# Moving the last unit's value convolution and gated product from the up stage into the down stage of a decoder layer

## The reference, cut to what matters

```
h = rmsnorm(x, norm_ffn_pre)
up = causal_depthwise_conv(h @ w_up, conv_w, conv_b)   # 3 taps: y[t] = b + w0*h[t-2] + w1*h[t-1] + w2*h[t]
gate, val = up[..., :D_FF], up[..., D_FF:]             # D_FF = 2816
f = (silu(gate) * val) @ w_down
x = x + rmsnorm(f, norm_ffn_post)
```

## Time and profile before

| | |
|---|---|
| runs | 2508.09, 2510.10, 2510.82 us; median 2510.1 us |
| the profiled execution's own time | 2507.04 us |
| its span (first to last instruction) | 2505.4 us |
| mean granted clock of TensorE | 0.978 |
| PE busy, share of the span | 94% |
| DVE, ACT, POOL busy | 73%, 49%, 40% |

### The profile page before, as it was taken

The page is one execution under the profiler, slowest core; times in us unless marked ns, Lnnn a source line. Parts: engine busy times, 40 slices in busy tenths (PEclk is TensorE's granted clock), DMA queues, the critical chain, the costliest instruction groups (busy, mean ns, idle before and its releaser), DMA issues. The chain is left out here.

```text
span 2505.4 us, 37528 instructions
## 1 busy us (share of the span) xinstructions
PE 2350.7 (94%) x11661; PEld 1950.1 (78%) x11661; DVE 1830.5 (73%) x2141; ACT 1226.5 (49%) x2101; POOL 1005.9 (40%) x747
## 2 busy tenths in 40 slices
PE   6989999989999979996999999899999989999987
PEld 5767887878888877884888888678888868888865
DVE  4424222989999976887998998999999963344687
ACT  4412112879898974555444444544444433333444
POOL 0000001786666642556454554455454520121463
PEclk9999999999999999997999999999999999999999
DMA  7932337143333315778233332633233334445566
GB/s 232 289 89 75 127 117 198 55 127 85 87 95 89 90 35 159 236 217 260 85 105 100 109 105 84 206 101 105 84 113 105 96 114 151 160 175 174 173 208 240
DMA packets 297728, 341.53 MB, mean 136 GB/s; under 512 B 13508, under 2 KB 219004, under 8 KB 292476
## 3 DMA queue, kind: packets, MB, share of 16 engines
q1 hardware_dynamic: 295292, 331.50, 42.9%
q0 software_dynamic: 2304, 8.39, 0.8%
HBM read 213.48 MB, written 109.58 MB: 129 GB/s over the span
## 5 line engine op out<-in xcount | busy, mean ns | idle before, releaser
L764 POOL TENSOR_TENSOR weight<-beta,stick 128x512 f32<-128x512 f32 (+3 forms) x320 | 304.2, 958 | 572.0 <-ACT beta L717 450.8
L1968 DVE SCALAR_TENSOR_TENSOR x<-up_cols,taps,x 128x1024 f32<-128x1024 f32 x176 | 259.2, 1473 | 16.2 <-ACT x L1870 13.0
L811 DVE TENSOR_TENSOR_SCAN stick<-z_ps,stick,beta 128x512 f32<-128x512 f32 x192 | 245.5, 1279 | 10.9 <-ACT z_ps L718 9.7
L540 PE MATMUL out_ps<-hT,w_hi 128*128 128x512 f32 x768 | 239.7, 393 | 9.8 <-DVE w_lo L474 9.8
L1955 DVE TENSOR_TENSOR wu_lo<-wu_sums,wu_hi 128x512 fp32r<-128x512 f32 x175 | 216.4, 1237 | 0.0
L717 ACT ACTIVATE beta<-z_ps 128x512 f32<-128x512 f32 (+3 forms) x320 | 171.2, 535 | 59.2 <-PE z_ps L841 52.5
L1857 ACT ACTIVATE wu_hi<-wu_sums 128x512 fp32r<-128x512 f32 x175 | 109.6, 628 | 170.0 <-PE gate_odd_ps L2079 91.1
L2079 PE MATMUL value_chain_ps<-wide,wu_hi 128*128 128x512 f32 x528 | 178.5, 392 | 9.9 <-DVE up_cols L2026 9.6
L540 PEld LDWEIGHTS out_ps<-hT,w_hi 128*128 128x128 f32 x768 | 145.2, 189 | 42.0 <-DVE w_lo L474 10.3
L858 PE MATMUL wT_ps<-ident,weight 128*128 128x128 f32 x1088 | 173.3, 275 | 3.1 <-POOL weight L764 3.1
L718 ACT ACTIVATE z_ps<-z_ps 128x512 f32<-128x512 f32 (+3 forms) x320 | 172.0, 538 | 0.0
(11 more groups left out here) (239 smaller groups left out, 6201.5 us busy)
## 6 DMA issues: line engine op xcount, KB each, us to landing
wu_f<-in_w_up SPq DMA_DIRECT2D x44, 512.0 KB, 4.9
bridge<-in_w_up SPq DMA_DIRECT2D x44, 512.0 KB, 4.9
f_scratch<-f_sum SPq DMA_DIRECT2D x88, 256.0 KB, 2.0
down_lo<-f_scratch SPq DMA_DIRECT2D x44, 512.0 KB, 3.3
down_b<-in_w_down SPq DMA_DIRECT2D x76, 256.0 KB, 3.7
f_scratch<-x SPq DMA_DIRECT2D x66, 256.0 KB, 2.1
x_scratch<-x SPq DMA_DIRECT2D x56, 256.0 KB, 2.8
first_head<-qk_scratch SPq DMA_DIRECT2D x24, 512.0 KB, 9.7
```

The lines of the kernel that those rows point to most:

```text
L540: m = pe.matmul(out_ps[half + j][:, :], w[slot][:, k, :], hT[h][:, k, j * BANK:(j + 1) * BANK], start=(k == 0 and t == 0), stop=(k == kc - ...
L764: pool.tensor_tensor(weight[v % weight_ring][:, 0:w], beta[v % stick_in][:, 0:w], stick[q % 2][:, at:at + w], ALU.mult).then_inc(weight_do ...
L811: dve.tensor_tensor_scan(stick[q % 2][:, at:at + w][:, ::-1], backwards, beta[u % stick_in][:, 0:w], start, ALU.mult, ALU.bypass).then_inc ...
L1968: dve.scalar_tensor_tensor(out=conv[h], in0=cols[:, h, 2 - back:2 - back + span], scalar=column(kind, h, e), in1=conv[h], op0=ALU.mult, op ...
```

## The change

It alters where and when five things of the last unit are done.

- ACT copies the high parts of the down stage's first operands inside the last unit, ahead of its SiLU, and no longer behind the value tap.
- DVE subtracts to get their low parts behind the last gate convolution and ahead of `value_even`, which is now DVE's last instruction of the up stage.
- The last value tap opens ACT's program of the down stage; the two shifted taps open DVE's. The product f follows on DVE behind `split(1)`, with new semaphores `last_tap`, `last_conv` and `last_f`.
- POOL waits for `last_f` before its four sums. SP stores the last f and its four sums behind load 5 (they were stored at the end of the up stage and ahead of load 3). ACT waits for `last_f` at step 11, before it writes into memory that the last `cols` may share.
- `cols` and `taps` are allocated in `build`, ahead of the other left-side tiles of `phase_up`. For the three new semaphores, SP clears those of the first stage's name group too, at the start of the attention stage.

```
@@ phase_down
+        last_tap, last_conv, last_f = (n.sem(x) for x in ("last_tap", "last_conv", "last_f"))
...
+                def store_last_f():
+                    sp.wait_ge(last_f, 1)
+                    for half, operand in enumerate(("a12", "a22")):
+                        sp.dma_start(s["f7"][F_OPERANDS.index(operand), n_k - 1][:, BANK:],
+                                     down["f"][1][:, half * BANK:(half + 1) * BANK]).then_inc(f_out[1], 16)
+                    for k, (i, operand) in enumerate(F_SUM_ORDER):
+                        sp.wait_ge(f_sum_done, 4 * (units // 2) + k + 1)
+                        sp.dma_start(s["f7"][F_OPERANDS.index(operand), n_k - 1][:, BANK:], down["f_sum"][:, i, :]).then_inc(s_out, 16)
...
-                for k, (i, operand) in enumerate(F_SUM_ORDER):
-                    sp.wait_ge(f_sum_done, 4 * (units // 2) + k + 1)
-                    sp.dma_start(s["f7"][F_OPERANDS.index(operand), n_k - 1][:, BANK:], down["f_sum"][:, i, :]).then_inc(s_out, 16)
                 for g in range(3, len(steps)):
                     p, k = steps[g]
                     load(g)
+                    if g == 5:
+                        store_last_f()
...
             def _(pool):
+                pool.wait_ge(last_f, 1)
                 f_sums(pool, down["f"], down["f_sum"], f_sum_done, 4 * (units // 2))
...
+                def last_value_tap():
+                    act.activation(down["conv"][1], down["cols"][:, 1, 2:], ACT.Identity, scale=down["taps"][:, 1, 3, 1, :],
+                                   bias=down["taps"][:, 1, 0, 1, :]).then_inc(last_tap, 1)
+
+                last_value_tap()
                 act.sem_inc(sq_done, n_t)
                 for g, (p, k) in enumerate(steps):
+                    if p == 1 and k == 0:
+                        act.wait_ge(last_f, 1)
                     if g:
                         half(g)
...
+                def last_value_conv():
+                    conv, cols, taps = down["conv"][1], down["cols"], down["taps"]
+                    for i, (back, kind) in enumerate(((1, 2), (2, 1))):
+                        if i == 0:
+                            dve.wait_ge(last_tap, 1)
+                        else:
+                            dve.wait_ge(last_conv, 1)
+                        dve.scalar_tensor_tensor(out=conv, in0=cols[:, 1, 2 - back:2 - back + 2 * BANK], scalar=taps[:, 1, kind, 1, :],
+                                                 in1=conv, op0=ALU.mult, op1=ALU.add).then_inc(last_conv, 1)
+
+                def last_f_product():
+                    dve.wait_ge(last_conv, 2)
+                    dve.wait_ge(f_out[1], stored(units // 2 - 1, 32))
+                    dve.wait_ge(f_sum_done, 4 * (units // 2))
+                    dve.tensor_tensor(down["f"][1], down["conv"][0], down["conv"][1], ALU.mult).then_inc(last_f, 1)
+
+                last_value_conv()
                 for g, (p, k) in enumerate(steps):
                     if g:
                         split(g)
+                    if g == 1:
+                        last_f_product()
@@ phase_up
-        cols = n.sb("up_cols", [P, 2, 2 + span])
+        cols, taps = down["cols"], down["taps"]
...
-        taps = n.sb("taps", [P, 2, 4, 2, 1])
...
                 sp.dma_start(down["b_f"], a["w_down"][0][0:P, 0:BANK]).then_inc(start_in, 16)
-                sp.wait_ge(f_done, units)
-                store_odd(parts - 1, n_ff // 2 - 1)
                 sp.wait_ge(start_in, 32)
...
+                    if last:
+                        act.wait_ge(start_in, 32)
+                        act.activation(down["hi"][:, 0:a["d"]], as_f32(down["lo"][:, 0:a["d"]]), ACT.Copy).then_inc(start_hi_done, 1)
+                        act.activation(down["hi"][:, a["d"]:], down["b_f"], ACT.Copy).then_inc(start_hi_done, 1)
                     act.wait_ge(gate_conv, 2 * u + 2)
                     act.activation(conv[0], conv[0], ACT.Silu).then_inc(silu_done, 1)
...
                 units_of(act, unit)
-                value_tap(units - 1, 1)
-                act.wait_ge(start_in, 32)
-                act.activation(down["hi"][:, 0:a["d"]], as_f32(down["lo"][:, 0:a["d"]]), ACT.Copy).then_inc(start_hi_done, 1)
-                act.activation(down["hi"][:, a["d"]:], down["b_f"], ACT.Copy).then_inc(start_hi_done, 1)
...
                 units_of(dve, unit)
-                value_even(units - 1, 1)
-                dve.wait_ge(value_even_done, units)
-                shifted(1, 1, value_tap_done, units - 1, value_conv)
-                f_of(units - 1, 1, units // 2 - 1)
                 dve.wait_ge(start_hi_done, 1)
                 dve.tensor_tensor(down["lo"][:, 0:a["d"]], as_f32(down["lo"][:, 0:a["d"]]), as_f32(down["hi"][:, 0:a["d"]]), ALU.subtract)
                 dve.wait_ge(start_hi_done, 2)
                 dve.tensor_tensor(down["lo"][:, a["d"]:], down["b_f"], as_f32(down["hi"][:, a["d"]:]), ALU.subtract)
+                value_even(units - 1, 1)
@@ build
-                retired += phase_values(nc, a, c, s, hT, start, w_first, bridge)
+                retired += phase_values(nc, a, c, s, hT, start, w_first, bridge) + f.made
...
+        cols, taps = m.sb("up_cols", [P, 2, 2 + 2 * BANK]), m.sb("taps", [P, 2, 4, 2, 1])
```

More of the change, by code:

```diff
@@ L1646, in phase_up @@
         sums = up_start["sums"]
-        cols = n.sb("up_cols", [P, 2, 2 + span])
-        conv = [x8[:, 2 * i:2 * i + 2, :, :].rearrange("p b c t -> p (b c t)") for i in range(2)]
+        cols, taps = down["cols"], down["taps"]
+        conv = down["conv"]
         f, f_sum = down["f"], down["f_sum"]
@@ L2194, in build @@
         phase_mix(nc, a, c, s, wide, bridge, up_start)
+        cols, taps = m.sb("up_cols", [P, 2, 2 + 2 * BANK]), m.sb("taps", [P, 2, 4, 2, 1])
         flat = [up_start[x][:, :, :, :].rearrange("p h c n -> p (h c n)") for x in ("a_hi", "a_lo")]
-        down = {"hi": flat[0], "lo": flat[1], "b_f": up_start["w_f"][:, 0, 0:half, :].rearrange("p c n -> p (c n)"), "f_sum": n.sb("f_sum", [P, 4, BANK], side="right"),
+        down = {"cols": cols, "taps": taps, "conv": [up_start["x8"][:, 2 * i:2 * i + 2, :, :].rearrange("p b c t -> p (b c t)") for i in range(2)],
+                "hi": flat[0], "lo": flat[1], "b_f": up_start["w_f"][:, 0, 0:half, :].rearrange("p c n -> p (c n)"), "f_sum": n.sb("f_sum", [P, 4, BANK], side="right"),
                 "f": [up_start["x8"][:, 4 + 2 * i:6 + 2 * i, :, :].rearrange("p b c t -> p (b c t)") for i in range(2)],
```

## The result

| | before | after |
|---|---|---|
| median of 22 runs | 2509.76 us | 2513.77 us |
| lowest, highest | 2505.62, 2513.96 us | 2509.40, 2518.02 us |
| profiled execution, its span | 2507.04, 2505.4 us | 2511.74, 2510.1 us |

The ratio is 1.0017, with a 95% interval of 1.0011 to 1.0024: the changed kernel is slower by about 4 us, where 6.65 us less was forecast. The time is outside the range given.

A forecast was written before the change was run, and what follows sets the result against it. PE bounds the kernel, working for 94% of the span. Step 1 starting 6.5 to 6.8 us earlier, taken as 6.65, and nothing for the rest gave 2510.1 - 6.65 = 2503.5 us; range 2501.0 to 2506.8 us.

The forecast's parts named there:

- The gap: PE's wait between up and down stage: 2.1 us in place of 8.1, the down stage starting 5.96 us earlier.
- rival 4: Up stage's end: the block's end waits for something else, ACT the candidate through a late SiLU; 2510; chance 0.04.
- Step 0 and its clock: Down stage's first step: 5.45 us at full clock, 7.1 us if half clock follows the gap; the clock decides little.
- its two cases: Step 0 at full clock, then a wait of 1.3 us, or slowed by half clock to 7.1 us.
- Step 1: Down stage's second step: starts at S + 6.8 to S + 7.1, 6.5 to 6.8 us earlier, taken as 6.65.
- S: Start of the down stage after the change, forecast at 2047.06 in place of 2053.02.
- rival 3: Down stage's start: the moved convolution delays step 1; with 4 us more, 2.7 us saved, 2507.4 us; chance 0.06.
- The rest of the down stage: Behind step 1: moved sums, stores and waits cost nothing, all later waits shifting as a whole.
- POOL's four sums: Down stage, waiting for f: four of 1.27 us from S + 8.0 to S + 13.1, costing nothing.
- The failed step: Semaphore clears and moved tiles: taken as nothing, with 0 below and 2.6 us above for the clears.
- rival 5: All 44 units: new tile addresses slow matmuls or splits; at 0.35 us a unit 8.8 us lost, 2518.9 us; chance 0.05.
- rival 1: The forecast itself, at the stage handover: 6.65 us saved, bounds 5.9 to 7.6 us; chance 0.76.

The follow-up runs named there:

- e1: The changed kernel with 32 bytes of padding behind `taps`; 2507.4 us, ratio 0.9998 to the kernel before.
- e5: The changed kernel with `cols` and `taps` on the right side of SBUF, the moved tiles at their old addresses; 2501.5 us, ratio 0.9975 to the kernel before.
- e6: As e5, with 64 bytes of padding on the right side ahead of `x8`; 2490.5 us, ratio 0.9924 to the kernel before.
- e8: As e5, but DVE makes the down stage's first low parts behind `value_even` again; 2503.6 us in one run, the kernel before 2507.7.
- e4: The kernel before plus a final block of PE-only matmuls, operands offset by 0 to 224 bytes; 226.7 ns between starts at fast distances, 232 to 234 at slow.
- e7: The probe of e4 with other operand distances, up to 1024 bytes; 226.7 ns between starts at 256, 512 and 1024, 232 to 234 at slow distances.
- e9: As e5, but last value tap, shifted taps and f stay in the up stage; 2506.9 us in one run, the kernel before 2507.7.

## Why the prediction was wrong, point by point

- **The gap.** Right: 2.1 us forecast, 2.05 measured. The end of the block stayed at about 0.3 us, SiLU was not late: it started at 2054.80, 0.04 us behind the end of DVE's gate taps, with ACT's copies ahead of it (the first at 2050.96). So rival 4 is out.
- **Step 0 and its clock.** Right that it matters little. The granted clock of step 0 is 1.00 after the change, and all 24 matmuls run in 5.5 us (columns as in rows 8):

```profile
2057.40:2062.90 5.50, 5.47 (x24) 4.43 (x24) 2.57 (x2) 2.15 (x2) 0.00 (x0) 1.00 0.67 223
```

  In e1 the half clock came behind a gap of nearly the same length, 2.04 us (granted clock 0.50 from 2057.7 to 2060.7), and its handover is 9.8 us, no longer than after's 10.0. So which of its two cases would come, the prediction could not tell from the gap; it was right to give the clock little weight. The rule cited there from the Trainium skill (TensorE: Matmul & The Clock Gate, "HAM oscillation — how this bites in real kernels"), by which so short a gap leaves PE at full rate, held in after, e5 and e6, and failed in e1 and e8.
- **Step 1.** Forecast at S + 6.8 to 7.1, measured at S + 7.54 (2064.97 - 2057.43), which is past the limit that the prediction set itself; S + 7.0 in e5 and e6, S + 7.3 in e1. SP's issue comes at +0.63 in place of +0.29, and the high parts start 3.93 us behind it in place of 3.49, when load 1 has landed. The gain was forecast 0.5 us too large by this (6.65 for 6.13). The taps did not delay it: DVE was idle for 1.79 us ahead of step 1's low parts, and ACT for 3.33 us ahead of the high parts, so rival 3 is out.
- **The rest of the down stage.** Nothing was lost at loads 6 to 8. From step 1 to the end it is 444.7 us before and 445.1 after. Two terms were too small and cost nothing: POOL's four sums took 1.6 to 2.3 us each in place of 1.27, and DVE's low parts beside them up to 1.78 us (L1560) in place of 0.69; PE waited for neither.
- **The failed step** is "Six more semaphores cleared by SP and tiles at other addresses: the trace of before has no row for either. I take nothing." The addresses cost 10.5 us in the up stage, 0.24 us in each of the 44 units, where the forecast wanted the stage's length as before. The clears cost nothing that shows: the up stage starts at the same time in both, and e5 has them and gains 6.2 us. This is rival 5 in its place and nearly at its threshold (0.26 us a unit for over 0.2% slower), and it had been given 0.05. The sum with it: -6.1 + 10.5 = +4.4 us, measured +4.0. That the change looks almost harmless, 0.17%, is the accident of a gain and a loss of like size.
- A row for it was in the trace of before all the same, and "no row" was wrong: matmuls of one shape in one stage took 389 ns with some tiles and 396 with others. All had the same form, and PE waited for nothing. The prediction did not look at that split; it would have been the place to ask what moving tiles does.
- **Two sums in the rivals.** In rival 1, with step 1 at S + 5.9 the saving is 5.96 + 7.64 - 5.9 = 7.7 us, not 7.6. In rival 4, the 5.7 us do not come out of the rows: SiLU could end 2052.71 - 2045.44 = 7.3 us later before the stage starts no earlier than it did. Neither touches the forecast.

## What to carry to other kernels

Adding or moving a buffer is an edit of every tile allocated behind it. Before such a change, and after it, compare the mean time of matmuls of one shape by tile: where two groups differ by some ns with PE never idle, look at the remainders by 256 bytes of the addresses of weights and moving operand, and pad until they agree. Here this was worth more (10 to 11 us) than the change under study (6 us), and a pad of 64 bytes did it. It was tried with fp32r matmuls of 128x512 alone; for other types and shapes it is a thing to measure, not a rule.

## What the runs showed of the hardware that was not expected

- Matmuls of 128x512 in fp32r at full clock follow each other every 226.7 ns if weights and moving operand start at the same remainder by 256 bytes within a partition. Otherwise it is 229 ns (moving operand 64 bytes above) or 232 to 234 ns. This holds with all other engines idle (e4, e7). The distances tried are multiples of 32 bytes, up to 1024; why it is so the traces don't show. In e1 the product `s3t3`, two thirds of whose matmuls have a distance of 128, took 230 ns, less than this gives; that stays open.
- In the kernel before the slow distance has an after-effect: the first six matmuls of the well-placed product behind a badly placed one (`s2t2` behind `a12b21`) still start 228 to 236 ns apart, the next six 226.7. After the change `a22t4`, whose operands moved together and stay well placed, went from 229 to 231 ns among badly placed neighbours. In e6, where all are well placed, all 84 of a unit have 226.1 to 227.2.
- A PE gap of 2.04 to 2.06 us between the stages was followed by half clock in one of four runs (for about 3 us in e1; not in after, e5, e6), one of 2.78 us (e8) by 6 us of it, and one of 7.37 us (e9) by only 3 us. The length of the gap alone does not say what the clock does.
